# Two decoder stacks in one kernel: out-projections and last down groups by token halves, shorter norm chains, up tiles one by one

## What is computed

```python
for l in (0, 1):                                  # first block
    h = rms_norm(x, g_pre_mix[l]) * (1.0 + sc_m) + sh_m
    y = token_mixer(h, ...)                       # projections, two kinds of attention, @ w_out
    x = x + gt_m * rms_norm(y, g_post_mix[l])
    h = rms_norm(x, g_pre_ffn[l]) * (1.0 + sc_f) + sh_f
    a = causal_depthwise_conv(h @ w_up_act, w_conv, b_conv)
    y = (gelu(a) * (h @ w_up_lin)) @ w_down       # D_FF 2816
    x = x + gt_f * rms_norm(y, g_post_ffn[l])
```

## Time and profile before

| what | us |
|---|---|
| median of 3 runs (2807.65 to 2808.84) | 2808.84 |
| the profiled execution: its time | 2810.76 |
| the profiled execution: its span | 2808.9 |
| PE busy, share of the span | 2589.0, 92% |
| DVE busy | 1732.7, 62% |
| ACT busy | 1261.1, 45% |
| POOL busy | 672.4, 24% |
| mean granted clock of PE | 0.952 |

### The profile page before, as it was taken

The page is one execution under the profiler, slowest core; times in us unless marked ns, Lnnn a source line. Parts: engine busy times, 40 slices in busy tenths (PEclk is TensorE's granted clock), DMA queues, the critical chain, the costliest instruction groups (busy, mean ns, idle before and its releaser), DMA issues.

```text
span 2808.9 us, 36584 instructions
## 1 busy us (share of the span) xinstructions
PE 2589.0 (92%) x14371; PEld 2095.4 (75%) x14371; DVE 1732.7 (62%) x1989; ACT 1261.1 (45%) x1294; POOL 672.4 (24%) x353
## 2 busy tenths in 40 slices
PE   5998999898799897899897679999999999999996
PEld 3874898785799664799775468787888888787884
DVE  0153565543775554765556377777777777777776
ACT  1122443223443112333211157776677776776763
POOL 0000000000930250860053113222223233232223
PEclk7998999999899998999997789999999999999998
DMA  9886675366585463695431169999999999999993
GB/s 309 260 272 211 207 231 158 126 194 201 193 264 173 133 232 101 222 264 180 150 104 61 62 233 352 347 350 348 341 355 332 367 329 366 331 349 348 345 354 124
DMA packets 434952, 693.80 MB, mean 247 GB/s; under 512 B 37690, under 2 KB 255894, under 8 KB 434838
## 3 DMA queue, kind: packets, MB, share of 16 engines
q1 hardware_dynamic: 407456, 677.09, 70.3%
q10 hardware_dynamic: 27382, 15.10, 1.9%
HBM read 691.10 MB, written 1.05 MB: 246 GB/s over the span
## 4 chain that ended last, share of the span: by engine, by line
PE 50%; issue 29%; POOL 11%; DVE 6%; ACT 2%; DMA 1%; SPq 1%; POOLq 0%; ACTq 0%; DVEq 0%
POOL ring_part L1166 10%; PE bank L602 9%; PE bank L725 8%; PE bank L727 8%; PE bank L726 8%; PE bank L719 3%; PE bank L548 3%; PE bank L616 2%; PE bank L816 1%; PE bank L531 1%; PE bank L665 1%; PE bank L836 1%; PE bank L697 1%; SPq L1085 1%; POOL stat L1198 1%
## 5 line engine op out<-in xcount | busy, mean ns | idle before, releaser
L1275 ACT ACTIVATE region_part<-ring 128x2048 fp32r<-128x2048 f32 x432 | 806.0, 1907 | 279.7 <-PE bank L727 170.4
L727 PE MATMUL bank<-ring_part,region_part 128*128 128x512 f32 x1648 | 648.8, 394 | 0.0
L2052 DVE TENSOR_TENSOR ring_part<-ring,region_part 128x2048 fp32r<-128x2048 f32 x270 | 640.3, 2404 | 1.6 <-ACT region_part L1275 1.5
L725 PE MATMUL bank<-region_part 128*128 128x512 f32 x1432 | 582.1, 407 | 6.2 <-DVE ring_part L2052 6.2
L726 PE MATMUL bank<-region_part 128*128 128x512 f32 x1296 | 511.6, 395 | 0.0
L1166 POOL TENSOR_TENSOR ring_part<-ring,region_part 128x2048 fp32r<-128x2048 f32 x54 | 268.3, 4976 | 554.9 <-ACT region_part L1275 554.9
L727 PEld LDWEIGHTS bank<-ring_part,region_part 128*128 128x128 f32 x1648 | 309.6, 188 | 71.3
L725 PE MATMUL bank<-xn_part,region_part 128*128 128x256 f32 x1152 | 327.2, 284 | 22.0 <-DVE hT_part L2090 11.3
L727 PE MATMUL bank<-hT_part,region_part 128*128 128x256 f32 x1152 | 325.8, 283 | 0.0
L726 PE MATMUL bank<-xn_part,ring_part 128*128 128x256 f32 x1152 | 325.8, 283 | 0.0
L725 PEld LDWEIGHTS bank<-region_part 128*128 128x128 f32 x1432 | 269.4, 188 | 75.5 <-issue 14.6
(11 more groups left out here) (286 smaller groups left out, 3404.9 us busy)
## 6 DMA issues: line engine op xcount, KB each, us to landing
ring<-in_moe_w_gate SPq DMA_DIRECT2D x126, 1024.0 KB, 5.1
ring<-in_moe_w_up SPq DMA_DIRECT2D x126, 1024.0 KB, 5.2
ring<-in_moe_w_down SPq DMA_DIRECT2D x126, 1024.0 KB, 5.0
ring<-in_w_ada SPq DMA_DIRECT2D x48, 1024.0 KB, 7.4
ring<-in_mod_w SPq DMA_DIRECT2D x48, 1024.0 KB, 5.4
ring<-in_w_in SPq DMA_DIRECT2D x44, 1024.0 KB, 5.5
ring<-in_w_up_act SPq DMA_DIRECT2D x22, 1024.0 KB, 5.4
ring<-in_w_up_lin SPq DMA_DIRECT2D x22, 1024.0 KB, 6.0
```

The source lines that it names most:

```text
L725: nc.tensor.matmul(o, split(a_hi), split(b_hi), start=start, stop=False, skip_group_check=True)
L727: return nc.tensor.matmul(o, split(a_hi), split(b_lo), start=False, stop=stop, skip_group_check=True)
L1275: return nc.scalar.activation(out_, in_, func, **kw).then_inc(*done(*event))
L2052: v.tensor_tensor(split(w), w, whole(hi), ALU.subtract).then_inc(*done("moe_lo", j, e))
```

## The change

- `out_projection`: all four n for the tiles of token half t = 0 first, then all four again for t = 1. A new event ("pe_used", "y", l, "mix") marks the first half; ("pe_used", "out", l, n) is raised in the second half.
- `ffn`: the last two down groups (`last_downs`) likewise, t = 0 of both groups and then t = 1. `up(g)` finishes tile f = 2g with both m before tile 2g + 1, and ACT and DVE handle a tile at a time. The columns and `gate_half` products come one group earlier, the last one thereby before the last down groups. In the last group the down chunk's parts are made ahead of the tiles.
- `post_root`: for one t after the other; DVE multiplies y by the gate while ACT squares it, and one operation scales that and adds it to x. `post_gain` (gate by gain) comes ahead of it. `post_layer` goes by t as well.
- `norm_split` (layers 0 to 2): high and low part of hT by pairs of feature groups; PE starts on the first pair.
- Order of ACT and DVE ahead of the feed-forward: up g0 m0 before the y chain, up g0 m1 behind its larger part.
- `first_projections` (layer 1): the first two projection chunks on token half 0 between the transposes of the two halves.
- Start: c and ident are loaded first and by SP, x first by ACT; x is normed and transposed among the `ada` sums; the other constants, the gate bias and the rows are loaded after the first norm.

```diff
             def out_projection(l):
-                    for k in range(2):
-                        kk = 2 * n + k
-                        for i in range(4):
-                            t, c = i // 2, i % 2
...
-                    m.then_inc(*done("pe_used", *key))
+                for n in range(4):
+                    pe.wait_ge(*loaded(("out", l, n)))
+                    m = part(n, (0,))
+                m.then_inc(*done("pe_used", "y", l, "mix"))
+                for n in range(4):
+                    part(n, (1,)).then_inc(*done("pe_used", "out", l, n))
...
                 def up(g):
+                    for i in range(2):
+                        o = bank(("up", l, 0, 2 * g + i), ("up_out", l, 0, 2 * g + i), up_banks)
+                        for m, key in enumerate(keys):
+                            if i == 0:
+                                pe.wait_ge(*until("w_lo", *key))
...
+                                if (g, m, i, k % 2) == (0, 0, 0, 0):
+                                    pe.wait_ge(*until("hT_lo", l, k // 2))
...
+                def last_downs(gs):
+                    for t in range(NT):
+                        for g in gs:
+                            pe.wait_ge(*until("w_lo_down", l, g))
+                            for f in (2 * g, 2 * g + 1):
+                                last = down_part(f, t)
...
+            def first_projections(l):
...
+                turned(0)
+                hT_half(0)
+                half(0, 0)
+                turned(1)
+                half(1, 0)
+                hT_half(1)
+                half(0, 1)
+                half(1, 1)
...
# ACT, ahead of a feed-forward
-                    for m in (0, 1):
-                        leading(("up", l, 0, 0, m))
+                    leading(("up", l, 0, 0, 0))
                 if l < 2:
-                    post_squares(l, "mix")
+                    post_squares(l, "mix", 0)
+                    squares(l, "ffn", (0,))
+                    post_squares(l, "mix", 1)
+                if l < 3:
+                    leading(("up", l, 0, 0, 1))
                 if l < 2:
-                    squares(l, "ffn")
-                norm_out(l, "ffn")
+                    squares(l, "ffn", (1,))
+                if l < 3:
+                    norm_split(l)
...
# DVE
                 scales(l, "ffn")
+                if l < 2:
+                    post_gain(l, "mix")
                 if l < 3:
-                    for m in (0, 1):
-                        rest(("up", l, 0, 0, m))
+                    rest(("up", l, 0, 0, 0))
                 if l < 2:
                     post_root(l, "mix")
...
+                for t in range(NT):
+                    after()
+                    dve.wait_ge(*until(*y_ready(l, stage, t)))
+                    for c in (1, 0):
+                        sl = slice(c * 512, (c + 1) * 512)
+                        if c == 0:
+                            dve.wait_ge(*until("y_ssq", l, stage, 2 * t))
+                        v.tensor_tensor(xn[:, t, sl], psum[bank_of["y", l, stage, 2 * t + c]], gate[:, sl], ALU.mult)\
...
+                    dve.wait_ge(*until("rstd", l, "post", stage, t))
+                    v.scalar_tensor_tensor(x[:, t, :], xn[:, t, :], stat[:, 42 + t:43 + t], x[:, t, :], ALU.mult, ALU.add)\
...
# start, PE
-            for q in range(8):
+            for q in range(6):
                 ada_sum(0, 0, q, 0)
...
+            ada_sum(0, 0, 6, 0)
+            norm_tiles(0, "mix")
+            ada_sum(0, 0, 7, 0)
```

More of the change, by code:

```diff
@@ L570, in norm_tiles @@
                 free = (0, 1, 2, 4) if stage == "ffn" else (0, 1, 2, 3)
-                tiles = [bank(("norm", l, stage, b), ("hT", l, stage, b) if b % 2 == 0 else ("hTd", l, stage, b), (free[b],))
-                         for b in range(4)]
+                tiles = [bank(("norm", l, stage, b), norm_free(l, stage, b), (free[b],)) for b in range(4)]
                 for t in range(NT):
@@ L749, in up, with down_part @@
                                 last.then_inc(*done("pe_used", "up", l, g))
+                def down_part(f, t):
+                    key = ("down", l, 0, f // 2)
+                    w, wh = chunk(key), hi_part(key)
+                    pe.wait_ge(*until("up_out", l, 0, f))
+                    ts = slice(t * P, (t + 1) * P)
+                    for c in range(2):
+                        cs = slice(c * 512, (c + 1) * 512)
+                        last = product(tiles[2 * t + c], hf_hi[f % 4][:, ts], hf[:, f % 4, ts], wh[:, f % 2, cs], w[:, f % 2, cs],
+                                       f == 0, f == FF[l] // P - 1)
+                    return last
                 def down(g):
@@ L1551, in ffn @@
             def ffn(l):
-                act.wait_ge(*until("hTd", l, "ffn", 3))
-                act.wait_ge(*done.prev())
-                for i in range(2):
-                    run(split(hT_hi[:, 4 * i:4 * i + 4, :]), hT[:, 4 * i:4 * i + 4, :], ACT.Copy, "hT_hi", l, i)
                 groups = ffn_groups(l)
@@ L1663, in _ @@
                 if l < 2:
-                    post_squares(l, "ffn")
+                    for t in range(NT):
+                        post_squares(l, "ffn", t)
+                        if l == 0:
+                            squares(1, "mix", (t,))
         @block.vector
@@ L1874, in attention, with post_gain @@
                 acc_out(l + 1, "mix", ADA_MIX - 1)
+            def post_gain(l, stage):
+                gate = mod_gate[:, 0 if stage == "mix" else 1 + l % 2, :]
+                dve.wait_ge(*until(f"rows_{stage}{l}", 0))
+                after()
+                v.tensor_tensor(gate, gate, rows[:, 0, :], ALU.mult).then_inc(*link())
             def post_root(l, stage):
@@ L1879, in post_root @@
                 nl, nstage = (l, "ffn") if stage == "mix" else (l + 1, "mix")
-                dve.wait_ge(*until(f"rows_{stage}{l}", 0))
-                after()
-                v.tensor_tensor(gate, gate, rows[:, 0, :], ALU.mult).then_inc(*link())
-                def own(t):
+                for t in range(NT):
+                    after()
+                    dve.wait_ge(*until(*y_ready(l, stage, t)))
[4 more added lines that the diff above has]
+                        v.tensor_tensor(xn[:, t, sl], psum[bank_of["y", l, stage, 2 * t + c]], gate[:, sl], ALU.mult)\
+                            .then_inc(*(done("y_gated", l, stage, t, 1) if c else link()))
```

396 lines of the change are left out of this document (235 added, 161 removed).

## The result

| | before | after |
|---|---|---|
| median, us | 2808.84 (4 runs, 2807.65 to 2810.80) | 2772.45 (4 runs, 2771.36 to 2772.58) |
| ratio to before, with its 95% interval | | 0.9869 (0.9852 to 0.9886) |
| span of the profiled execution | 2808.9 | 2770.6 |
| forecast of the median | | 2769.0 (2757.0 to 2789.0) |

The account below looks back on a forecast made before the run. PE was taken as bound by the untouched mixture of experts and by waits at stage changes (ten, 57 us). Terms summed to -40.2: 2810.76 to 2770.6, less 1.9 for the median, 2769; own range 2761 to 2777, overall 2757 to 2789.

Parts of the forecast that it names:

- The start: Start to first projection: deferred loads bring the last ada sum and first projection earlier, -8.5 us; bounds 5 and 11 gained.
- The term behind it: Start: 8.6 us from last ada sum to first projection, 4.6 for columns and scales, about 4 for evacuation with its hop.
- The load of up g0 m0 as what holds the chain: Layers 0 and 1, mixer to feed-forward: late load delays the norm, +3.0; totals -3.4 and -6.0, bounds +1 and -13 each.
- The second gap: Before the second up group, layers 0 and 1: 3.27 and 5.81 us vanish, up g0 m1 being made during chain waits.
- rival c: Layers 0 and 1: the late load doesn't hold the first half, each gains another 9.5 us, 2750; chance 0.06.
- The ends of the feed-forwards: Layers 0, 1, 2: the second half's products cover the first half's chain; -6.3, -5.3, -4.9 us, bounds -2 and -8.
- Layer 2: Layer 2, mixer to feed-forward: order by t adds 0.9 of hops, pairs give 1.9 back; -1.0 us, bounds -3 and +2.
- The pairs give 1.9 back: Layer 2, before the first up product: starting on pairs of hT's feature groups regains 1.9 us.
- Rivals a: Ten table groups, layers 1 and 2: DVE waits behind POOL, 0.5 to 1.5 us each; 2779, chance 0.15.
- b: All transitions: overlaps are worth half because added hops between engines eat the cover; 2789, chance 0.13.
- d: Inside the feed-forwards' 36 groups: one-tile order makes each group wait; at 1.5 us per group 2823, chance 0.03.
- e: All transitions: the change moves waits and keeps their sum; 2807, chance 0.03.

Follow-up runs that it names:

- e6: Changed kernel with gate biases and tables loaded by ACT's queue ahead of the norm again; 2772.84 us, first projection at 41.74 instead of 37.79.
- e1: Changed kernel with both chunks of up g0 ahead of the four ada chunks in the plan of loads; 2771.95 us.
- e5: Changed kernel with both chunks of up g0 loaded behind the first two of the four ada chunks; 2745.06 us, ratio to the kernel before 0.9769.
- e9: Kernel of e5 with the out-projection undone (all four tiles together, no halves); 2770.14 us.
- e4: Changed kernel with the two tiles of an up group filled together and handled in pairs by ACT and DVE again; 2786.08 us.
- e3: Changed kernel with the last two down groups undone, both halves of y ready only at the last product; 2784.76 us.
- e8: Changed kernel without layer 1's first projections on half the tokens, all 16 transposes coming first; 2772.0 us.
- e10: Kernel before the change with nothing but the load plan of e5; 2806.97 us, ratio 0.9993.
- e12: Kernel of e5 with layer 2's hT split in two halves of four feature groups, as in the kernel before; 2747.94 us.
- e7: Changed kernel with the first norm's 16 transposes behind the last ada sum; first projection at 40.70, +2.9 us; no total given.
- e2: Changed kernel with the out-projection undone (all four tiles together, both halves of y ready only at its end); 2771.32 us.

## Why the prediction was right, and where it was not

**The start, -8.5 forecast, -11.9 measured.** The bytes were right: the last ada sum came at 32.96 (32.5 forecast), and e6 gives 3.95 us for 1.43 MB. The term behind it was mis-sized: 8.6 from the last sum to the first projection is 4.83 in the rows above, and so the gain lies outside the bound of 11. The forecast took 4.6 to the scales and about 4 for the evacuation with its hop. The scales are done at 35.75, 2.8 us behind the start of the last sum:

```profile
35.58 0.17 DVE L1861 SCALAR_TENSOR_TENSOR scale_col<-mod_col,pcol 128x8 f32<-128x8 f32 x1
```

Two things of the kernel before had been left in the 4.6. The six transposes of the parameters (1.54 us on PE behind the last sum) now stand before it, and everything on PE from that sum to the first projection ran at 1.2 GHz before; this was in the trace and I didn't read it. The rest, from the scales to the first projection, is 2.0 and not 4. The 15 us from the last sum on, in the kernel before and in the changed one (us, busy us by engine, PEclk, DMA share, GB/s):

```profile
38.00:53.00 15.00, 11.05 (x50) 8.70 (x51) 5.08 (x12) 5.04 (x10) 1.11 (x2) 0.50 1.10 345
```

```profile
33.00:48.00 15.00, 11.84 (x71) 8.96 (x71) 3.36 (x8) 2.53 (x5) 0.00 (x0) 0.89 1.09 360
```

**Layers 0 and 1.** The load of up g0 m0 as what holds the chain: right in each step, and e1, e5 and e9 show it as the cause. +3.0 was +2.6. The second gap: the amount was right and the reason wrong, as e4 shows; the step that failed is "up g0 m1 is made during the chain's own waits, so I take the gap as gone". It did not hurt because the other edit closed the gap; that was luck. Without it the two feed-forwards take 14.9 us more (e4).

**The bound of -13 and rival c.** Hiding the half was priced at 9.5 us for each of two layers. e5 gives 10.1 (17.86 to 7.79 and 17.97 to 7.83), and 8.9 in layer 2, which c had left out.

**The ends of the feed-forwards and layer 3.** -5.3, -5.0, -4.6 and -4.8 against -5.3, -4.2, -4.9 and -4.8. The first three make 14.9. The last two down groups are worth 16.6 (e3) and the first projections 2.35 (e8). If the two add, that is 4 us more than the gain, so other parts of the change cost as much at these ends. The chain by t is a candidate: without the halves it is 2.2 and 2.6 us longer in layers 0 and 1 and 0.9 in layers 2 and 3 (T to N, e9 against e10).

**Layer 2.** -1.0 forecast, +3.2 measured, outside the bounds of -3 and +2. The 0.9 of hops came (T to N +0.8). "The pairs give 1.9 back" is the term that failed: the first up product comes 3.32 us behind N instead of 3.77, so they gave 0.45, where each of DVE's low parts takes three times as long beside POOL. Behind the first product another 2.8 us were lost (253.61 for 250.77), which the forecast put at nothing and whose cause stays open: e12 made the low parts shorter and won none of it. For the length of the low parts the rule of the Trainium skill that the forecast weighed ("SBUF — State Buffer", section "SBUF: two separate sides") was the better guide, as 2097 ns for 685 show: I set it aside for the table groups, rightly by their rows, and didn't look where else POOL reads SBUF during a chain.

**Rivals a, b, d and e.** None came. The table groups cost nothing that can be told: layer 1, with five of them (POOL is busy 88.6 of the 199 us), takes 199.12 us from the first up product to T, layer 0, with none (0.55), 199.30, and for those of layer 2 e4 says the same. The rivals of half the overlap and of waits that only move are refuted by the pieces.

**The rest goes with the clock.** -3.4 (layer 3's mixer) and +2.7 (the last products) lie in code that the change doesn't touch, and +2.3 in layer 1's out-projection, where the order of the matmuls isn't the cause, as the list below shows. That these add to only +1.6 is luck, and so is that the start (3.4 more than forecast) and layer 2 (4.2 less) all but cancel: the total is closer than its terms. The windows (us, busy by engine, then PEclk, DMA share, GB/s) of layer 1's out-projection, the first 42 us behind N in layer 2, layer 3's mixer, and the end, in the changed kernel:

```profile
647.50:677.50 30.00, 29.98 (x67) 13.01 (x67) 0.00 (x0) 1.41 (x1) 0.00 (x0) 0.92 0.29 90
1103.00:1145.00 42.00, 36.52 (x263) 33.29 (x264) 31.96 (x26) 18.46 (x18) 40.82 (x42) 0.84 0.46 153
1370.00:1519.90 149.90, 126.71 (x621) 96.20 (x621) 92.95 (x172) 28.86 (x57) 62.09 (x50) 0.88 0.23 78
2738.00:2770.00 32.00, 7.11 (x8) 1.60 (x8) 19.27 (x22) 0.90 (x2) 5.75 (x4) 0.55 0.08 33
```

The same in e8 for the out-projection, and in the kernel before for the other three:

```profile
649.40:677.20 27.80, 27.77 (x68) 12.19 (x72) 0.00 (x0) 1.64 (x1) 0.00 (x0) 1.00 0.31 98
```

```profile
1135.00:1177.00 42.00, 36.32 (x283) 33.51 (x284) 33.35 (x24) 18.41 (x16) 40.82 (x42) 0.91 0.55 181
1404.20:1557.40 153.20, 129.49 (x620) 97.53 (x620) 92.85 (x172) 29.11 (x58) 61.98 (x50) 0.85 0.23 76
2779.00:2809.00 30.00, 4.50 (x8) 1.19 (x8) 19.25 (x22) 0.86 (x2) 5.75 (x4) 0.70 0.09 35
```

At the end PE's eight products take 4.50 us in the kernel before and 7.11 in the changed one, in the mixer all of PE's work 129.5 and 126.7. The 64 matmuls of that out-projection took 27.7 us in seven of the fourteen kernels (the one before, e1, e3, e4, e6, e8, e10) and 29.9 to 30.0 in the other seven. Both lengths occur with the halves (e1, e3; e5, e7) and without them (before, e10; e2, e9). Each kernel has one trace, so whether the length belongs to the kernel or to the execution is not shown; executions of one kernel differ by up to 6.8 us (e4, 2780.55 to 2787.37).

## What to carry to other kernels

Work that hides beneath a product can be held back by a transfer that the product itself has to release: before halving anything, list what each of the waiting engines has ahead of it in order, and in which half its buffer's event now falls. When an experiment on such a suspect leaves the time as it was, cut the span into pieces before dropping the suspect: e1 moved 29 us out of three places and lost 26 in three others, and one more look at the order of slots turned that into a version 27 us faster than the change. Before cutting an operation into smaller ones, look whether another engine slows it there: each piece may cost nearly as much as the whole.

## What the runs showed of the hardware

- A DVE subtraction with two sources in SBUF, 128x512: 685 ns with POOL idle, 2097 on average while POOL works through 128x1024 products; 128x1024 in the same place: 2760, and 1220 with POOL idle (layer 0 of the kernel before). Four small ones cost 8.2 us, two large ones 5.4, for the same elements.
- The out-projection of layer 1 stands at one of two lengths, 27.7 or 29.9 to 30.0 us, with a granted clock of 1.00 or of 0.92 to 0.93 over it. In e6 and e7, which differ from the changed kernel in the start alone, it took one length and the other. In e9 layer 0's out-projection took 27.74 us at 1.00; in the other kernels it took 29.4 to 30.1. Differences of 2 to 3 us in a stretch are no evidence in this kernel unless the clock of the stretch, or its scatter over other kernels, is beside them.
